# A Mamba-2 scan in a two-layer encoder: three elementwise products moved from GpSimd to VectorE

## The reference

```python
xdt = (x * dt[..., None])                                      # products with the step sizes
cb = einsum('bclgn,bcsgn->bcgls', Cc, Bc)
m = cb[:, :, :, None] * segsum_exp(a)                          # decay between two positions of a chunk
y_diag = einsum('bcgrls,bcsgrp->bclgrp', m, xdt)               # inside a chunk of 128
decay_states = exp(a_cs[..., -1:] - a_cs)
states = einsum('bclgn,bclgrp->bcgrpn', Bc, xdt * decay_states[..., None])   # what a chunk hands on
y_off = einsum('bclgn,bcgrpn->bclgrp', Cc, prev) * decay_out[..., None]      # what a chunk receives
y = y_f + y_b + xs * D_skip[:, None]                           # both directions, and the skip with D
y = y.reshape(b, l, SSM_INNER) * silu(z)
```

## Time and profile before

| | |
|---|---|
| median of 3 runs | 1644.38 us (1639.74 to 1646.62) |
| the profiled execution | 1639.83 us, of which the span on the core is 1638.1 us |
| TensorE (PE) busy | 1527.2 us, 93% of the span |
| VectorE (DVE) busy | 1063.9 us, 65% |
| ScalarE (ACT) busy | 788.4 us, 48% |
| GpSimd (POOL) busy | 410.4 us, 25% |
| the three products on GpSimd | L1095 x64 58.7 us, L1078 x16 21.1 us, L1103 x16 20.2 us |
| mean granted TensorE clock | 0.976 of full speed |

### The profile page before, as it was taken

One profiled execution on the slowest core, in us unless ns is written; L12 is line 12 of the kernel. 1 busy time (PEld: TensorE's weight loads), 2 busy tenths in 40 slices (PEclk: granted clock), 3 DMA queues, 4 the chain that ended last, 5 costly groups with the idle time before them and its releaser, 6 DMA issues.

```text
span 1638.1 us, 30327 instructions
## 1 busy us (share of the span) xinstructions
PE 1527.2 (93%) x11327; PEld 1454.0 (89%) x11327; DVE 1063.9 (65%) x1352; ACT 788.4 (48%) x1077; POOL 410.4 (25%) x227
## 2 busy tenths in 40 slices
PE   4999887989989999999999998888998899999997
PEld 4899787868978999999999987786898899999997
DVE  5544569998887646554443555999888874565543
ACT  4444557754333445444444545676433344454453
POOL 3310000022212144454434000001221213354442
PEclk9999999999989999999999999999999999999998
DMA  5544333443333455656545434344433245555552
GB/s 175 186 143 135 117 104 105 140 141 105 119 113 113 154 172 162 198 174 218 175 156 178 138 117 129 103 120 128 139 117 103 90 155 181 168 171 189 187 201 101
DMA packets 149140, 238.39 MB, mean 146 GB/s; under 512 B 11665, under 2 KB 57611, under 8 KB 149003
## 3 DMA queue, kind: packets, MB, share of 16 engines
q1 hardware_dynamic: 147339, 235.11, 45.6%
q10 hardware_dynamic: 1664, 1.48, 0.3%
HBM read 235.50 MB, written 1.05 MB: 144 GB/s over the span
## 4 chain that ended last, share of the span: by engine, by line
PE 56%; DVE 20%; DVEq 10%; ACT 7%; issue 5%; ACTq 2%; DMA 1%
PE PS L498 51%; DVE wL L1150 5%; PE S L498 4%; DVE regA L1374 3%; ACT wH L806 3%; DVEq L1371 2%; DVE actL L1394 2%; DVEq L1416 2%; DVEq L1397 1%; DVE scr L1414 1%; DVE actH L1394 1%; DVE small L1332 1%; DVEq L1331 1%; ACT scr L923 1%; ACTq L974 1%
## 5 line engine op out<-in xcount | busy, mean ns | idle before, releaser
L1150 DVE TENSOR_TENSOR wL<-w_raw,wH 128x1024 fp32r<-128x1024 f32 (+1 forms) x330 | 472.9, 1440 | 368.7 <-ACT wH L806 353.7
L806 ACT CAST wH<-w_raw 128x1024 fp32r<-128x1024 f32 (+1 forms) x443 | 453.4, 1041 | 250.2 <-PE PS L498 219.5
L498 PE MATMUL PS<-hH,wH 128*128 128x256 f32 x1856 | 544.8, 294 | 4.1 <-DVE wL L1150 4.1
L498 PE MATMUL PS<-hL,wH 128*128 128x256 f32 x1856 | 534.2, 288 | 0.0
L498 PE MATMUL PS<-hH,wL 128*128 128x256 f32 x1856 | 534.0, 288 | 0.0
L1066 POOL TENSOR_TENSOR wL<-w_raw,wH 128x1024 fp32r<-128x1024 f32 (+1 forms) x113 | 297.2, 2634 | 438.2 <-ACT wH L806 438.2
L498 PEld LDWEIGHTS PS<-hH,wH 128*128 128x128 f32 x1856 | 365.8, 197 | 11.3 <-issue 6.4
L498 PEld LDWEIGHTS PS<-hL,wH 128*128 128x128 f32 x1856 | 365.7, 197 | 1.9 <-issue 1.4
L498 PEld LDWEIGHTS PS<-hH,wL 128*128 128x128 f32 x1856 | 365.3, 197 | 0.0
L498 PE MATMUL PS<-actH,wH 128*128 128x256 f32 x1120 | 324.7, 290 | 8.3 <-DVE wL L1150 2.9
L498 PE MATMUL PS<-actH,wL 128*128 128x256 f32 x1120 | 319.2, 285 | 0.0
(11 more groups left out here) (231 smaller groups left out, 1603.4 us busy)
## 6 DMA issues: line engine op xcount, KB each, us to landing
w_raw<-in_w_in_dram SPq DMA_DIRECT2D x192, 512.0 KB
w_raw<-in_w_ffn_in_dram SPq DMA_DIRECT2D x176, 256.0 KB
w_raw<-in_w_branch_dram SPq DMA_DIRECT2D x64, 512.0 KB
w_raw<-in_w_ffn_out_dram SPq DMA_DIRECT2D x44, 512.0 KB
w_raw<-in_w_mem_kv_dram SPq DMA_DIRECT2D x35, 512.0 KB
w_raw<-in_w_out_dram SPq DMA_DIRECT2D x16, 512.0 KB
regA<-in_mem_dram SPq DMA_DIRECT2D x6, 512.0 KB, 5.1
scr<-in_x_dram ACTq DMA_DIRECT2D x1, 1024.0 KB, 11.1
```

Source lines behind the costliest of these rows:

```text
L498: return nc.tensor.matmul(o, l, r, start=first, stop=last, skip_group_check=True)
L806: nc.scalar.copy(wH[:, slot].rearrange("p k c -> p (k c)")[:, q], raw[:, slot].rearrange("p k c -> p (k c)")[:, q]).then_inc(h_done[slot], 1)
L1150: v.tensor_tensor(wL[:, slot].rearrange("p k c -> p (k c)")[:, q], raw[:, slot].rearrange("p k c -> p (k c)")[:, q], wH[:, slot].rearrange ...
```

## The change

The three products leave GpSimd's list and stand in VectorE's, in the same steps of the same table:

- `decay` on VectorE first makes the two products of 128x256 (`xdt`), after a wait for `diag_done` that GpSimd had, then waits for the exponential and goes on as before.
- `scale` and `off` become steps of VectorE, one product of 128x512 each.
- The semaphore `xsd_done` and its wait in `assemble` go, as do GpSimd's waits. The operands and the sizes are the same. Nothing changes in the lists of TensorE, ScalarE and SyncE, nor in which low parts GpSimd makes.

In a layer these are 32 products of 128x256 and 16 of 128x512.

```diff
@@ block.gpsimd
-            def step(lay, kind, i):
-                if kind == "scale":
-                    g, c = i // 2, i % 2
-                    if i > 0:
-                        pool.wait_ge(off_done, 8 * lay + i)
...
-                elif kind == "decay":
-                    if i == 0:
-                        pool.wait_ge(xs_ready, 8 * lay + 8)
-                        pool.wait_ge(dt_ready, lay + 1)
-                        pool.wait_ge(conv_done, 6 * lay + 6)
-                        pool.wait_ge(da_yt, 4 * lay + 4)
-                    if i >= 2:
-                        pool.wait_ge(diag_done, 16 * lay + i - 1)
...
-                elif kind == "off":
-                    if i > 0:
-                        pool.wait_ge(y_done, 8 * lay + i)
...
-                each_step(lambda u, g, c: split_l(lay, u + LOOKAHEAD), group_end, lambda *s: step(lay, *s), ffn_loop)
+                each_step(lambda u, g, c: split_l(lay, u + LOOKAHEAD), group_end, lambda *s: None, ffn_loop)
@@ block.vector
+                elif kind == "scale":
+                    g, c = i // 2, i % 2
+                    if i > 0:
+                        dve.wait_ge(off_done, 8 * lay + i)
+                    q = 64 * (1 - c) + SH * (1 - c) + HPG * g
+                    v.tensor_tensor(v3(xw, HPG), v3(xsN[:, 1 - c, UC * g:UC * (g + 1)], HPG),
+                                    gains(wgt[:, q:q + HPG], HPG, DH), ALU.mult).then_inc(xw_done, 1)
+                elif kind == "off":
+                    g, c = i // 2, i % 2
+                    v.tensor_tensor(v3(xsd, HPG), v3(xsN[:, c, UC * g:UC * (g + 1)], HPG),
+                                    gains(r_D[:, HPG * g:HPG * (g + 1)], HPG, DH), ALU.mult)
                 elif kind == "decay":
-                    c = i // 2 % 2
+                    g, c, hf = i // 4, i // 2 % 2, i % 2
+                    if i == 0:
+                        dve.wait_ge(xs_ready, 8 * lay + 8)
+                    if i >= 2:
+                        dve.wait_ge(diag_done, 16 * lay + i - 1)
+                    at = UC * g + 256 * hf
+                    for d in range(2):
+                        q = pair_heads(i, d)
+                        ins = v.tensor_tensor(v3(xdt[hf][d], 4), v3(xsN[:, c, at:at + 256], 4),
+                                              gains(dtv[:, q:q + 4], 4, DH), ALU.mult)
+                    ins.then_inc(xdt_done, 1)
                     dve.wait_ge(exp_done, 16 * lay + i + 1)
...
                     dve.drain().then_inc(side_free[2], 1)
-                    dve.wait_ge(xsd_done, 8 * lay + i + 1)
                     v.tensor_tensor(ytmp, ytmp, xsd, ALU.add)
```

More of the change, by code:

```diff
@@ L334, in build @@
         xdt_done = sem("ssm_xdt")
-        xw_done, off_done, xsd_done, y_done, st_done, sd_done, n_done, yt_done, g_done, gh_done, ssm_y = (
-            sem("ssm_" + n) for n in ("xw", "off", "xsd", "y", "st", "sd", "n", "yt", "g", "gh", "out"))
+        xw_done, off_done, y_done, st_done, sd_done, n_done, yt_done, g_done, gh_done, ssm_y = (
+            sem("ssm_" + n) for n in ("xw", "off", "y", "st", "sd", "n", "yt", "g", "gh", "out"))
         sg_used, br_done = sem("sg_used"), sem("br_done")
@@ L1069, in split_l @@
                                         ALU.subtract).then_inc(l_done[slot], 1)
-            def step(lay, kind, i):
-                if kind == "scale":
-                    g, c = i // 2, i % 2
-                    if i > 0:
-                        pool.wait_ge(off_done, 8 * lay + i)
[L1077 to L1080, removed]
-                elif kind == "decay":
-                    g, c, hf = i // 4, i // 2 % 2, i % 2
-                    if i == 0:
-                        pool.wait_ge(xs_ready, 8 * lay + 8)
-                        pool.wait_ge(dt_ready, lay + 1)
-                        pool.wait_ge(conv_done, 6 * lay + 6)
-                        pool.wait_ge(da_yt, 4 * lay + 4)
-                    if i >= 2:
-                        pool.wait_ge(diag_done, 16 * lay + i - 1)
[L1092 to L1097, removed]
-                elif kind == "off":
-                    g, c = i // 2, i % 2
-                    if i > 0:
-                        pool.wait_ge(y_done, 8 * lay + i)
-                    nc.gpsimd.tensor_tensor(v3(xsd, HPG), v3(xsN[:, c, UC * g:UC * (g + 1)], HPG),
-                                            r_D[:, HPG * g:HPG * (g + 1)].unsqueeze(2).broadcast_to([P, HPG, DH]),
-                                            ALU.mult).then_inc(xsd_done, 1)
             for u in range(LOOKAHEAD):
```

## The result

The changed kernel took 1647.44 us (median of 16 runs, 1642.84 to 1653.01), the kernel before 1642.48 us beside it (16 runs, 1637.98 to 1646.62). The ratio is 1.0034 with a 95% interval of 1.0023 to 1.0045: 5.6 us more, where +7.2 were forecast. It is slower by less than the 0.5% that the chances use as their bound, so it falls under "no change".

A forecast was written before the change was run, and what follows sets the result against it. VectorE was taken to bound the scan's body B (with A and D), TensorE A2 and C. Terms -0.9 + 3.9 + 0 + 0.6 = +3.6 us a layer, +7.2 on 1644.38, gave 1651.6 us; range 1638 to 1662.

The forecast's parts named there:

- The sum: Whole kernel: -0.9 + 3.9 + 0 + 0.6 = +3.6 us a layer, +7.2 us for both layers, 0.44%.
- A: Head of the first layer's scan, 335.0 to 342.3 us: VectorE's lengthening goes, so TensorE goes on 2.1 us earlier.
- A2: Next 24.2 us of the scan, bound by TensorE up to the exponential: with A together -0.9 us.
- B: Body of the scan, 366.5 to 505.3 us, VectorE's chain: +14.5 added, -10.6 lengthening removed, net +3.9 us a layer.
- the 0.5 us for the new waits: In B: 17 new waits on VectorE, satisfied long before, each costing a sequencer's gap of 0.03 us.
- C: Scan after B, to 532.4 us: VectorE's net +1.1 us hidden in its 2.25 us wait for ScalarE, so 0.
- D: End of the scan, to 560.9 us: the last `xsd` stands in the chain, +0.6 us a layer.
- the ratio of a third: VectorE's lengthening against GpSimd's product time in B, 10.6 to 33.0 us, used to price the lengthening in C.
- the clock: TensorE's half-speed stretch in C costs about 1.7 us a layer; a longer wait before it can't cost it twice.
- The gaps: Rival: each of 17 new waits in B shows a 0.20 us gap, 3.4 instead of 0.5; +13 us, 1657; chance 0.22.
- Hidden after all: Rival: TensorE truly bounds B, so added work vanishes there and A's 2.1 us stay; -4.2 us, 1640; chance 0.16.
- The lock: Rival: GpSimd's products in B hold VectorE up for all their 33.0 us; -12.6 us a layer, 1619; chance 0.12.

## Where the prediction was right, and where not

**The sum: right in its sign and its size, 1.6 us high.** +7.2 was forecast, the ratio gives +5.6, and its interval (3.8 to 7.4 us) takes in the forecast.

**A: right on VectorE, not passed on whole.** The 2.1 us came exactly. TensorE took less of them in layer 1: its idle time in A fell from 3.0 to 1.3 us, but part of the stretch ran at half clock, and it began A2 only 0.7 us earlier (10.53 us behind the convolution's last row instead of 11.20). In layer 2 it began A2 2.2 us earlier. TensorE in the changed kernel, layer 1:

```profile
335.93 0.50 PE L498 MATMUL PS<-wH,hH 128*128 128x512 f32 x1 [2.61 <-DVE wL L1114]
...
337.44 0.63 PE L498 MATMUL PS<-wH,hL 128*128 128x512 f32 x1
```

and in the kernel before:

```profile
336.20 0.50 PE L498 MATMUL PS<-wH,hH 128*128 128x512 f32 x1 [2.60 <-DVE wL L1150]
...
337.69 0.40 PE L498 MATMUL PS<-wH,hH 128*128 128x512 f32 x1
```

The granted clock of A is 0.75 after, 1.00 before, behind the same 2.6 us of idle time. In layer 2 no such stretch fell into A.

**A2: the number of layer 1 is luck, the mechanism shows in layer 2.** The forecast let the exponential come 2.1 us earlier and VectorE 0.7 later, so that VectorE was the later of the two and 0.9 of the 2.1 were left. In layer 1, 0.8 are left, but by another way: the exponential came only 0.8 earlier (TensorE had lost the rest to its clock), and VectorE, 0.3 later than before, still waited 0.48 us for it. In layer 2 VectorE is the later one, as forecast, but by 0.2 us and not 0.7, so 1.4 are left. The 0.5 between are terms that the forecast left out: two low parts of A and A2 were longer by 0.12 and 0.21 (1.35 at 340.85, and a pair of 2.57 at 362.40 instead of 2.36), and a gap of 0.21 ahead of the first decay went.

**B: the mechanism right, one term mis-sized.** The added 14.0 us stand (0.67 a pair, 0.60 each of the others). The lengthening removed was to be 10.6 and is 10.8. The step that failed is the 0.5 us for the new waits: VectorE's idle time in B fell by 0.3 instead. The groups show why. Ahead of L1414 1.1 us of sequencer's gaps stood before; ahead of L1401 there are none now, and 0.8 stand ahead of L1395. The pair took over the gap that the decay had, it did not add one; likewise the 0.4 and 0.3 ahead of L1379 and L1384 stand for 0.4 ahead of L1422 and 0.2 ahead of the `cb` before. That is 0.8 of the 1.0 us by which B was put too high.

**C and D: right.** 0 was forecast for C and +0.3 and -0.1 came; VectorE's wait for ScalarE in it fell from 2.25 to 1.28 us, so it hid 1.0 us where 1.1 were forecast. The 1.4 us of lengthening in that sum were worked out with the ratio of a third, which the experiments refute as a rule; by the rows it was 0.36 + 0.22 + 0.86 = 1.4 all the same, by luck. D was to be 0.6 longer and is, in both layers. The two kernels with `xsd` at this place on VectorE have a D of 26.9 us, the eight others 26.3. On the clock the forecast said that a longer wait can't cost it twice; yet behind the longer wait at the end of B the stretch at half clock is 6.83 us long (503.65 to 510.48, TensorE at work for 4.0 of them) where it was 3.41, and C's granted clock is 0.92 instead of 0.94.

**The rivals.** *The gaps* (slower, 1657): refuted, the waits cost nothing. *Hidden after all* (1640): refuted, B is 2.9 us longer, and TensorE's idle time in it grew from 10.4 to 15.0 us. *The lock* (faster, 1619) is half right, and that is the instructive part. Each meeting costs VectorE nearly the undisturbed length of the GpSimd product: 0.42 of 0.60 us, 0.84 of 1.04, and 2.19 (2.94 less 0.75) of 2.34 for the merging addition beside L1395. The rule of the Trainium skill's page "SBUF — State Buffer", section "SBUF: two separate sides", that the two engines exclude each other for a whole instruction, agrees with these steps to 0.2 us, and with the single meetings to 0.13 us (last section). What was wrong in the rival is that all 33.0 us counted. First, they contain GpSimd's own waiting: at 0.60 and 1.04 each, the 23 and 11 products are 25.2 us. Second, about 10 of those us cost B next to nothing: six of the 23 `xdt` products (0.13 us or less each) and all of `xsd`. The experiments that put GpSimd's work into VectorE's wait show this directly.

**What the forecast didn't see** is that its own rows held a better kernel. It priced the moved products at their full length because "the chain has no place here where VectorE waits for anything that it didn't release itself". That holds for the place they were moved to; but the loop over ScalarE behind each `assemble` is 2.0 us of VectorE's time with nothing in it, six times in B, and work put inside such a loop is free although VectorE released the loop itself.

**What stays open.** The 0.4 us of B that remain in the kernel with `xsd` back on GpSimd (1.8 gained, 3.0 - 0.83 = 2.2 accounted for); they are 0.4 more of VectorE's idle time (21.1 instead of 20.7) in several small gaps, and why these came isn't shown. The C of the ten profiled executions lies between 28.3 and 29.7 us without a tie to what was moved; I didn't work out the clock's part in that. Why TensorE ran at half clock in A in one layer and not in the other isn't explained either.

## What to carry to other kernels

Price work on GpSimd by its meetings, not by its busy time: lay both timelines side by side, find the VectorE instructions with two SBUF inputs that start while a GpSimd instruction runs, on the critical chain, and charge for each what is then left of the GpSimd instruction (for instructions in a row its undisturbed length less 0.2 us); where VectorE waits anyway the price is zero. Before moving such work to VectorE, look for the waits in which it could stand: the same products cost +0.34% in the ticks that use them and gave -1.0% behind the instruction that starts a 2 us loop over another engine. When a change gives back about as much as it costs, do its parts alone, and expect them not to add up: here `xw` was even, `xdt` lost 0.9 us because it pushed an `xsd` out of its wait, and `xsd`, free where it was, lost as much as the whole change.

## What the runs showed of the hardware that was not expected

The lengthening of VectorE comes in steps that depend on the GpSimd product met, +0.42 us for 128x256, +0.84 or 0.85 for 128x512, about +2.2 for 128x1024, and not on the size of VectorE's own instruction (+0.85 on a pair of 128x1024, 3.21 instead of 2.36). It is less where VectorE's instruction begins late in the product (0.13 at 375.20). The single rows of the traces give all of this one form: a VectorE instruction that starts while a GpSimd product runs is longer by what is left of the product at that moment, less 0.13 us. In the kernel before the `xw` at 384.62 ends at 385.66, and a low part starts at 384.88 with 0.79 us of it left and takes 1.87 instead of 1.21 (the shortest of its kind, +0.66); the `xw` at 407.39 has 0.98 left when a low part starts at 407.45, which takes 2.07 (+0.86). It holds within 0.02 us in 434 of the 455 such cases in the scans of the ten traces; most of the others are the scaling mentioned below (0.19 instead of 0.13) and starts with less than 0.13 left, which cost nothing. The same goes the other way: the low part at 427.68 started first and kept its 1.22 us, and the `xw` that came at 428.03 took 1.78 instead of 1.04. An instruction that reads one input from PSUM isn't held at all: L1422 at 537.15 keeps its 0.68 beside the `xsd` of 536.32, as do all 42 of its kind. The scaling of the normed y is held up too, though it reads only one large operand: 677 ns a product before, 480 in the changed kernel. It is mutual, since the `xdt` pair takes GpSimd 1.19 us alone and 2.00 beside the spread. And a stretch of TensorE at 1.2 instead of 2.4 GHz (0.63 instead of 0.40 us for a 128x512 matmul) followed 2.6 us of idle time in one execution and not in another with the same work ahead of it, and the head of that layer is 0.6 us longer than that of the other (34.69 and 34.12).
